# Weight loads, output weight pieces and the gate weights' split moved to later uses; queries and keys turned later; SP's sequence written out

## What is computed

```
u = rms_norm(x, gain);  q, k, v, gate = split(u @ w_in, 4)          # 8 heads of 128
q, k = rms_norm(q) * q_gain, rms_norm(k) * k_gain
z = (q @ k.T) * 128**-0.5                                           # per head, 1024 x 1024
weights[t, s] = sigmoid(z[t, s]) * prod over s < j < t of sigmoid(-z[t, j]),  for s < t
o = weights @ v
h = x + (o * silu(gate)) @ w_out
```

## Time and profile before

| | us |
|---|---|
| median of 3 runs | 1176.01 (1173.97 to 1178.4) |
| the profiled execution | 1174.98 |
| its span, first to last instruction | 1173.3 |
| TensorE busy | 1145.6 (98%) |
| VectorE busy | 831.4 (71%) |
| ScalarE busy | 419.7 (36%) |
| GpSimd busy | 162.5 (14%) |
| heads 0 to 5 of the attention (65.5 to 446.1) | 380.6 |

### The profile page before, as it was taken

The page is one execution under the profiler, slowest core; times in us unless marked ns, Lnnn a source line. Parts: engine busy times, 40 slices in busy tenths (PEclk is TensorE's granted clock), DMA queues, the critical chain, the costliest instruction groups (busy, mean ns, idle before and its releaser), DMA issues. The chain is left out here.

```text
span 1173.3 us, 19984 instructions
## 1 busy us (share of the span) xinstructions
PE 1145.6 (98%) x7012; PEld 1048.3 (89%) x7012; DVE 831.4 (71%) x1636; ACT 419.7 (36%) x887; POOL 162.5 (14%) x344
## 2 busy tenths in 40 slices
PE   8999999898999999999999999999999999999998
PEld 8999989898988989888888989898999999999787
DVE  5768786858687775774444778788888888788421
ACT  5554454444444444452222222323232322222200
POOL 2413131213122231110003100000000000000000
PEclk9999999999999999999999999999999999999999
DMA  8243545455454531066632110314242421107441
GB/s 251 56 120 113 172 145 183 154 149 185 145 173 136 153 99 46 1 237 209 208 108 72 55 37 19 115 67 137 74 141 71 135 84 45 46 37 292 153 139 72
DMA packets 145214, 141.78 MB, mean 121 GB/s; under 512 B 19936, under 2 KB 117472, under 8 KB 145120
## 3 DMA queue, kind: packets, MB, share of 16 engines
q1 hardware_dynamic: 106336, 120.88, 31.5%
q10 hardware_dynamic: 38784, 19.67, 6.2%
HBM read 93.86 MB, written 46.66 MB: 120 GB/s over the span
## 5 line engine op out<-in xcount | busy, mean ns | idle before, releaser
L28 PE MATMUL p_proj<-w_qkv_hi,ut_hi 128*128 128x384 f32 x504 | 171.9, 341 | 0.4 <-DVE ut_lo L911 0.4
L30 PE MATMUL p_proj<-w_qkv_hi,ut_lo 128*128 128x384 f32 x504 | 169.0, 335 | 0.0
L29 PE MATMUL p_proj<-w_qkv_lo,ut_hi 128*128 128x384 f32 x504 | 168.8, 335 | 0.0
L28 PE MATMUL p_proj<-w_ig_hi,next_hi 128*128 128x256 f32 x512 | 145.5, 284 | 0.0
L29 PE MATMUL p_proj<-w_ig_lo,next_hi 128*128 128x256 f32 x512 | 143.1, 279 | 0.0
L30 PE MATMUL p_proj<-w_ig_hi,next_lo 128*128 128x256 f32 x512 | 143.0, 279 | 0.0
L28 PE MATMUL p_proj<-next_hi,w_qf_hi 128*128 128x512 f32 x282 | 113.2, 401 | 0.0
L923 DVE TENSOR_TENSOR_SCAN a_skip<-a_skip,a_diagonal 128x641 f32<-128x641 f32 (+3 forms) x64 | 86.7, 1355 | 35.1 <-ACT a_beta L742 30.5
L30 PE MATMUL p_proj<-next_hi,w_qf_lo 128*128 128x512 f32 x282 | 110.1, 390 | 0.0
L29 PE MATMUL p_proj<-next_lo,w_qf_hi 128*128 128x512 f32 x282 | 109.9, 390 | 0.0
L28 PEld LDWEIGHTS p_proj<-w_ig_hi,next_hi 128*128 128x128 f32 x512 | 96.2, 188 | 0.0
(11 more groups left out here) (258 smaller groups left out, 2790.3 us busy)
## 6 DMA issues: line engine op xcount, KB each, us to landing
stage<-in_hg_w_in_dram SPq DMA_DIRECT2D x32, 512.0 KB, 4.6
stage<-in_sb_w_in_dram ACTq DMA_DIRECT2D x24, 512.0 KB, 5.3
w_out_hi_scratch<-m_in SPq DMA_DIRECT2D x32, 256.0 KB, 2.1
w_out_lo_scratch<-m_in SPq DMA_DIRECT2D x32, 256.0 KB, 2.5
m_in<-mixed_scratch SPq DMA_DIRECT2D x12, 448.0 KB, 6.0
a_gated<-in_x_dram SPq DMA_DIRECT2D x8, 512.0 KB, 3.9
m_in<-in_sb_w_out_dram SPq DMA_DIRECT2D x16, 256.0 KB, 3.4
ut_hi<-w_out_hi_scratch SPq DMA_DIRECT2D x8, 512.0 KB, 8.1
```

The lines of the kernel that those rows point to most:

```text
L28: pe.matmul(out, w_hi, m_hi, start=start, stop=False, skip_group_check=True)
L29: pe.matmul(out, w_hi, m_lo, start=False, stop=False, skip_group_check=True)
L30: return pe.matmul(out, w_lo, m_hi, start=False, stop=stop, skip_group_check=True)
```

## The change

- ScalarE's weight loads: q, k, v and gate columns of head h + 2 are loaded in step h after uses 4, 5, 6 and 7, one each. The loads of three after use 9, and those after use 9 of step -1, are gone. The number of loads is the same.
- The gate weights' split moves from use 5 to use 6 in PLAIN.
- The output weights are split after uses 4, 5, 7 and 8, not 0, 1, 5 and 6. SP loads the first two raw halves after position 1, not before position 0, and stores the pieces after positions 4, 5 and 7 and, the last one, after position 0 of the next head. Its wait for the stored parts stands after position 1 and no longer before the last read-back of a head.
- `turn_qk` stands at reduction step 5, not 2, in PLAIN.
- SP's loop over heads 1 to 4 becomes a sequence written out for heads 0 to 5.

```diff
--- before.py
+++ after.py
@@ -378,8 +378,9 @@
 
     IN_ORDER = [("qkv", i) for i in range(NAT)] + [("gate", half) for half in range(GATE)]
     GATE_EARLY = IN_ORDER[:6] + [("gate", 0), ("qkv", 6), ("qkv", 7), ("gate", 1)]
-    SPLIT_AT = [0, 1, 5, 6]
-    SPLITS_AFTER = {0: ("store", 0), 1: ("store", 1), 3: ("load", 2), 4: ("load", 3), 5: ("store", 2), 6: ("store", 3)}
+    SPLIT_AT = [4, 5, 7, 8]
+    SPLITS_AFTER = {4: [("store", 0)], 5: [("store", 1), ("load", 2)], 6: [("load", 3)], 7: [("store", 2)]}
+    TURN_AT = 5
     QUARTER = P // 4
     CARRIED = HEADS - 2
 
@@ -590,33 +591,37 @@
                     sp.wait_ge(w_ready[p], h)
                 load_columns(sp, stage, w_in, h, p).then_inc(w_loaded[p], 16)
 
-            def carry(h, k, group):
+            def carry(h, k):
 
                 sp.wait_ge(flipped, TILES * h + k + 1)
                 width = (tile_of(h, k) + 1) * P
                 sp.dma_start(flips[k, :, 0:width], skip[k % 2][:, 0:width]).then_inc(flip_stored[k % 2], 16)
                 sp.wait_ge(flip_stored[k % 2], 16 * (PAIRS * h + k // 2 + 1))
                 for c in range(2):
-                    if c == 1 and group is not None:
-                        for i in range(2):
-                            sp.wait_ge(link["w_parts_stored"][i], group * 64 + 64)
                     read_flipped(sp, h, k, c)
 
-            def carry_all(h, b, group, previous=None):
-
-                if group is not None:
-                    for i in range(2):
-                        load_raw_half(sp, m_in, w_out, link, group, i)
-                for j in range(TILES):
-                    carry(h, j, group if j == TILES - 1 else None)
-                    if j == 0 and previous is not None:
-                        store(previous, 1 - b)
-                    if group is not None and j in SPLITS_AFTER:
-                        what, part = SPLITS_AFTER[j]
-                        if what == "load":
-                            load_raw_half(sp, m_in, w_out, link, group, part)
-                        else:
-                            store_half(sp, m_in, w_out, link, group, part)
+            def carry_all(h, b):
+
+                group = h - 1
+                for k in range(TILES):
+                    carry(h, k)
+                    if k == 0 and h >= 1:
+                        store(h - 1, 1 - b)
+                    if k == 0 and group >= 1:
+                        store_half(sp, m_in, w_out, link, group - 1, 3)
+                    if k == 1 and group >= 0:
+                        if group >= 1:
+                            for i in range(2):
+                                sp.wait_ge(link["w_parts_stored"][i], group * 64)
+                        if group < 4:
+                            for i in range(2):
+                                load_raw_half(sp, m_in, w_out, link, group, i)
+                    if 0 <= group < 4:
+                        for what, part in SPLITS_AFTER.get(k, []):
+                            if what == "load":
+                                load_raw_half(sp, m_in, w_out, link, group, part)
+                            else:
+                                store_half(sp, m_in, w_out, link, group, part)
 
             def store(h, b):
                 sp.wait_ge(o_gated, PAIRS * h + PAIRS)
@@ -653,11 +658,8 @@
                 sp.dma_start(c["logits"][:, layer, :],
                              small_inputs["logits"][layer].rearrange("(h d) -> d h", d=P),
                              allow_slow_non_contiguous=True).then_inc(small_loaded, 16)
-            carry_all(0, 0, None)
-            with sp.Fori(0, 2) as pair:
-                for b in (1, 0):
-                    carry_all(pair * 2 + 2 - b, b, pair * 2 + 1 - b, pair * 2 + 1 - b)
-            carry_all(HEADS - 3, 1, None, HEADS - 4)
+            for h in range(CARRIED):
+                carry_all(h, h % 2)
             store(HEADS - 3, 1)
             for k in range(2):
                 load_mixed_early(sp, m_in, mixed, link, k)
@@ -832,14 +834,11 @@
                         act.activation(raw[t % 4][:, :, :],
                                        p_proj[i % 2][:, 0:3, :],
                                        ACT.Copy).then_inc(raw_ready, 1)
-                    if projects and i == (5 if plan is PLAIN else 3):
+                    if projects and i == (6 if plan is PLAIN else 3):
                         split_hi(n, 3)
                     if projects and i == 8 and not (isinstance(n, int) and n == HEADS - 1):
                         for p in range(3):
                             split_hi(n + 1, p)
-                    if plan is FIRST and i == USES - 1:
-                        for p in range(3):
-                            load(2, p)
                     if plan is SQUEEZED and i == USES - 1:
                         gate_sigmoids(n, nb, i, t)
                     attend(h, b, plan, "after", i)
@@ -851,11 +850,8 @@
                                        scale=-1.0)
                     if projects and kind == "gate" and not (plan is SQUEEZED and i == USES - 1):
                         gate_sigmoids(n, nb, i, t)
-                    if plan is PLAIN and i == 7:
-                        load(h + 2, 3)
-                    if plan is PLAIN and i == USES - 1 and not (isinstance(h, int) and h == HEADS - 3):
-                        for p in range(3):
-                            load(h + 3, p)
+                    if plan is PLAIN and 4 <= i <= 7:
+                        load(h + 2, i - 4)
                     if splits_rows(h) and i in SPLIT_AT:
                         split_half_hi(act, m_in, link, h - 1, SPLIT_AT.index(i))
 
@@ -1313,7 +1309,8 @@
                         for kt in range(KT):
                             if known_first(n) and i < TILES and kt == KT // 2:
                                 pe.wait_ge(ut_ready, 2 * i + 2)
-                            if i >= 3 and i % 2 == 1 and kt == (KT - 2 if plan is SQUEEZED and i == 9 else 2):
+                            if i >= 3 and i % 2 == 1 and kt == (KT - 2 if plan is SQUEEZED and i == 9 else
+                                                            TURN_AT if plan is PLAIN else 2):
                                 turn_qk(h, (i - 3) // 2, plan)
                             if known_first(n) and i + 1 < TILES and kt == KT // 2:
                                 turn_x(i + 1)
```

## The result

The changed kernel took 1192.62 us (1190.88 to 1193.58) against 1176.55 for the kernel before on the same chip: a ratio of 1.0137, interval 1.0113 to 1.016. The forecast was 1169.0, the range ended at 1176. The profiled execution took 1190.88 with a span of 1189.1, 15.8 more than before.

A forecast was written before the change was run, and what follows sets the result against it. TensorE was taken as the bound, losing 20.4 us to waits in six heads; 13.4 would remain at pair 1's outputs, so a gain of 7.0 takes the median from 1176.01 to 1169.0, range 1163 to 1176.

The forecast's parts named there:

- The outputs of pair 1: TensorE's wait for position 3's subtraction: 13.4 us still lost over six heads, of 20.4 lost before.
- The early start: Head start on VectorE: without three loads just ahead, heads 1 to 5 may start 1.8 us earlier, first scan near 2.8.
- The load beside position 3's read-back: Use 4's weight load, issued while position 3 is read back: charged 0.3 us a head, bounds 0 and 2.0.
- the slow rival: Use 4's load takes 2.0 us from position 3's read-back in every head: 1179.2, or 1184 with position 5's; chance 0.07.
- I cost them at nothing: Splits 2 and 3, behind uses 7 and 8, fall where VectorE waits for gate columns: no cost.
- 1.7 to spare: Pair 2: in head 3 position 5's subtraction ends 1.7 us before the outputs that need it start.
- if another output pair begins to wait: Sign in the profile after that would show the forecast wrong; no size given.
- Removing this wait alone wins nothing: Later transposes end their wait on the key tile, but TensorE reaches pair 1's outputs 1.2 us earlier and waits there.
- The gate weights' split and SP written out: Split one use later, still ahead of position 5's subtraction, and SP's loop as a written-out sequence: both charged nothing.
- The splits out of uses 0 and 1: Heads 1 to 4: two splits of 0.69 us leave VectorE's full queue, where they delay flips 1 and 2 by 1.4.
- The wait only moves: TensorE reaches pair 1's outputs sooner, the subtraction comes no sooner: gain 0 to 4 us, some 1174; chance 0.26.
- The weight loads get ahead: Use 4's load delays position 3's read-back by 2.0 us a head, loads and stores also position 5's: 1184; chance 0.07.

The follow-up runs named there:

- turn_only: The kernel before with only the queries' and keys' transposes moved from reduction step 2 to 5; ratio 1.0045 to the kernel before.
- pieces_only: The kernel before with only the output weights' splits, raw loads and part stores moved, SP written out for the new list; ratio 1.0001.
- after_pieces_back: The changed kernel with the places of the output weights' splits and SP's list and loop as before; ratio 1.0066 to the kernel before.
- padded: The kernel before with 60 more waits, all met already, at the head of TensorE's program; ratio 1.0013.
- sp_only: The kernel before with only SP's loop over heads 1 to 4 written out, order as before; ratio 1.0001.
- gate_only: The kernel before with only the gate weights' split moved from use 5 to use 6; ratio 1.0001.

## Why the prediction was wrong, step by step

**The outputs of pair 1: right in sum.** 13.4 was forecast as what stays lost there, 14.0 was measured. Two errors cancel in it: heads 1, 2 and 5 lost 1.8, 1.8 and 1.5 where 2.0 to 2.5 were charged, and heads 0, 3 and 4 lost 2.9, 2.7 and 3.3, where 1.8, 2.5 and 2.5 were. That the sum fits is luck.

**The early start: right in the main.** The first scans stand at 2.8, 2.8, 3.3, 3.7, 2.8 and 3.1 after the head's start, 2.8 forecast (heads 2 and 3 are 0.5 and 0.9 later), and the wait of pair 0 is gone.

**The load beside position 3's read-back: right.** From read issue to copy that took 4.2 to 4.6, and 4.2 to 4.5 before, so the term of 0.3 was fair and the slow rival's 2.0 was not there. The Trainium skill (DMA: Bandwidth & Descriptors, Queues, rings and completion order) has each DMA engine take descriptors in ring order, which put ScalarE's half of this read-back ahead of the load; these 4.2 to 4.6 agree with it.

**The trips of positions 4 to 7, which have no term in the sum: the step that failed.** The prediction charged the four loads at one place only, the read-back of position 3 (and in the rival, of position 5). What they met was the stores: positions 4 to 7 go out on SP's ring while a load runs on ScalarE's, and took 3.1 to 6.2 to land in heads 1 to 4, where it was 1.6 to 3.2, once 4.5 and once 4.7 before. These stores follow one another through SP, which waits for each, so a slow one delays the next; the moved part stores, which the forecast had no term for behind position 4, stand in that list. ScalarE waits for position 7's store ahead of 2.95 of weight splits, VectorE's 3.50 follow, and behind these comes one of the two piece splits of which the prediction said "I cost them at nothing": 0.6 of head 1's wait of 4.41. None of this was in the sum, whose walk ended at pair 2 with "1.7 to spare". Its own list of signs named it, "if another output pair begins to wait", without a case or a price for it. Pair 3's wait came of it, 11.4 in three heads, beside what the half clock behind it costs. Both halves are shown: the loads alone bring pair 3's wait, the change without them has none. The same page of the Trainium skill says that an engine of the DMA takes turns between rings packet by packet; that fits a small store that takes twice as long beside a big load, but no run shows the turns themselves. The prediction applied the rule to the read-backs and not to the stores.

**"Removing this wait alone wins nothing": the mechanism right, its price wrong.** The subtraction came no sooner and the wait moved, as said. But one wait of 3 is not two of 1.5: in heads 1 to 3 of turn_only it is followed by half clock, in head 4 it is not, and the pairs of about 1.5 in the profile before are not. Alone the move costs 0.45%, 5.3 of 1176, where it was held at nothing; that the clock is what costs is the reading above, not tested. No term of the sum had the clock, which was 1.00 in every slice before.

**The gate weights' split and SP written out: right**, 1.0001 each.

**The splits out of uses 0 and 1**: charged as a help to VectorE. Head 1 of pieces_only shows it, 1.5 shorter; heads 3 and 5 give it back at slow stores of their own (flip 1's takes 5.4 in head 5, beside the part stores that now stand there). Net 0 by the medians.

**The rivals.** "The wait only moves" is what turn_only shows, without the clock. "The weight loads get ahead" named the right DMAs and a wrong victim, with 1184 and 0.07. The range ended at 1176 since no case let pair 3 wait. By single parts, 0.80 for the loads, 0.45 for the transposes and nothing for the rest make 1.25%, against 1.37% measured; but the parts do not simply add, as taking out the pieces gives 0.7% and taking out the loads 1.1%.

## What to carry to other kernels

A load moved off one engine's queue is charged to every transfer that is in flight beside it, small stores above all, and then followed through each engine that waits for those in turn, down to the last consumer of the stage. Before two short waits of TensorE are merged, or one is lengthened, look at the clock: here no wait below about 1.9 was followed by half clock, and from 2.6 on nearly every one was; what that costs depends on whether TensorE sets the pace behind the wait. A single profile doesn't settle it: look at the mean clock of the other executions too. Loads issued a few instructions sooner in the same use gave the early start and won 0.5%.

## What the runs showed of the hardware

**Half clock behind a wait.** Over all thirteen kernels, heads 0 to 5: of 26 waits of 2.6 and more (start to start) 23 were followed by 3.4 or 6.8 at 0.50; of 12 between 1.9 and 2.4 five; of the shorter ones none. The three long ones without a fall are 3.03 and 3.24 in turn_only and 3.01 in after_pieces_back. So it is likely from the length of a wait, not certain. Within the 27 executions of the kernel before beside turn_only, the twelve with a mean clock of 1.0 have a median time of 1176.7, the five with 0.997 one of 1180.9: executions with more half clock are longer, though this doesn't tell the clock's cost from that of the longer wait ahead of it.

**Instruction fetch in the way of a read-back.** An engine's instructions come in by DMA too, in packets that the profile calls instruction. In head 0 the reads of position 1 are issued at 79.68 before and 79.59 after, yet ScalarE's copy stands at 83.46 and here:

```profile
84.60 0.85 ACT L773 ACTIVATE a_wt_hi<-a_beta 128x768 fp32r<-128x768 f32 x1 [2.81 <-DMA a_beta<-flips_scratch]
```

The DMA queues in the quarter microsecond 81.75 to 82.00 of the changed kernel (packets, MB, share of 16 engines) have one packet of instructions, which starts at 81.86 and takes one engine 0.95, beside the read-back's packets on ScalarE's queue, q10 (81.03 to 84.06):

```profile
q10 hardware_dynamic: 77, 0.05, 73.5%
q8 instruction: 1, 0.02, 23.7%
q1 hardware_dynamic: 23, 0.01, 15.7%
```

Before, it comes at 82.70, when the read-back's packets on q10 are nearly done (81.14 to 82.70):

```profile
q8 instruction: 1, 0.02, 26.2%
q10 hardware_dynamic: 6, 0.00, 4.7%
```

In the six kernels where this packet starts before 82.0 the copy stands at 84.4 to 85.0, in the three where it comes at 82.5 or later at 83.5 to 83.6; of three in between two are late (84.7) and one is not (83.2); in padded, where it is over (80.01 to 81.02) before the packets on q10 start at 81.88, reads and copy are 3.6 apart, and 3.8 before. So the trip is about 1.2 longer in nearly every kernel in which a fetch falls inside it. The 60 waits added to TensorE's program moved the packet 2.7 earlier, but it stands 0.2 and 0.9 earlier in sp_only and gate_only too, with TensorE's program untouched; whether the edit or another execution does that is not shown. In sp_only it makes 1.09 and 1.77 of waits in head 0 where 1.48 was; in the changed kernel, with the transposes later, the same 2.9 comes as one wait and is followed by half clock. That the packet is the cause rests on these coincidences; it was not moved by itself. The Trainium skill (Runtime: NRT & Kernel Launch, Instruction fetch mechanics) calls the cost of crossing from one block of instructions to the next mostly hidden. For TensorE that holds at this place, where it has no wait over 0.3 from 66 to 96 us in any of these kernels; for the read-back these coincidences speak against it.
